# Both halves of the gated one-hot matrix on VectorE, in the gate stage of an S5 + mLSTM + PEER block

## The reference, cut to what matters

```
def peer(h, w_query, key1, key2, expert_u, expert_v):
    ...
    top_s, pos = lax.top_k(cand, PEER_TOPK)
    experts = jnp.take_along_axis(cand_idx, pos, axis=-1)
    gates = jax.nn.softmax(top_s, axis=-1).astype(h.dtype)
    def block(args):
        tb, eb, gb = args
        u = jnp.take(expert_u, eb, axis=0)
        act = jax.nn.gelu(jnp.einsum('ted,td->te', u, tb)) * gb
        vv = jnp.take(expert_v, eb, axis=0)
        return jnp.einsum('te,ted->td', act, vv)
```

## Time and profile before

| | us |
|---|---|
| median of 3 runs | 4708.28 |
| lowest and highest | 4703.58, 4708.52 |
| span of the profiled execution | 4703.4 |
| TensorE matmul busy | 4432.6 (94%) |
| VectorE busy | 2598.8 (55%) |
| ScalarE busy | 1247.2 (27%) |
| GpSimd busy | 1132.2 (24%) |

### The profile page before, as it was taken

The page is one execution under the profiler, slowest core; times in us unless marked ns, Lnnn a source line. Parts: engine busy times, 40 slices in busy tenths (PEclk is TensorE's granted clock), DMA queues, the critical chain, the costliest instruction groups (busy, mean ns, idle before and its releaser), DMA issues.

```text
span 4703.4 us, 56133 instructions
## 1 busy us (share of the span) xinstructions
PE 4432.6 (94%) x19304; PEld 3596.4 (76%) x19304; DVE 2598.8 (55%) x3702; ACT 1247.2 (27%) x1346; POOL 1132.2 (24%) x680
## 2 busy tenths in 40 slices
PE   7999999967898999999888899999999999999997
PEld 4886666755786788887777788888888888888886
DVE  5228888476533445449999555555533433333334
ACT  3232222343222222223333222222222222222222
POOL 1003444432112444547676200000000000000001
PEclk9999999978999999999999999999999999999999
DMA  2332222421433232233444544444333332333322
GB/s 113 128 114 101 91 92 102 169 75 42 169 139 138 83 114 107 103 118 139 154 143 149 216 146 149 141 149 143 133 116 107 111 109 101 116 107 107 115 91 89
DMA packets 101020, 567.75 MB, mean 121 GB/s; under 512 B 12056, under 2 KB 12072, under 8 KB 48864
## 3 DMA queue, kind: packets, MB, share of 16 engines
q1 hardware_dynamic: 55872, 406.87, 24.4%
q0 software_dynamic: 24352, 93.07, 6.4%
q10 hardware_dynamic: 20736, 67.12, 3.7%
HBM read 487.30 MB, written 79.72 MB: 121 GB/s over the span
## 4 chain that ended last, share of the span: by engine, by line
PE 64%; DVE 14%; PEld 10%; issue 8%; ACT 1%; POOL 1%; DMA 1%; DVEq 1%; PEldq 0%; ACTq 0%; POOLq 0%; SPq 0%
PE mm L1615 10%; PE mm L1616 10%; PE mm L1617 10%; PE pv L1615 5%; PE pv L1616 5%; PE pv L1617 5%; PE sc L1615 5%; PE sc L1616 5%; PE sc L1617 5%; PEld mm L1615 2%; PEld mm L1617 2%; PEld mm L1616 2%; DVE hot_j L1520 2%; DVE hot_jg L1525 2%; DVE gst L1535 1%
## 5 line engine op out<-in xcount | busy, mean ns | idle before, releaser
L618 ACT ACTIVATE whi<-raw 128x2048 fp32r<-128x2048 f32 x380 | 726.9, 1913 | 948.4 <-PE sc L1617 800.0
L990 DVE TENSOR_TENSOR wlo<-raw,whi 128x2048 fp32r<-128x2048 f32 x293 | 672.1, 2294 | 534.0 <-ACT whi L618 532.7
L1615 PE MATMUL mm<-t_hi,whi 128*128 128x512 f32 x2048 | 809.5, 395 | 63.8 <-POOL wlo L513 59.1
L1616 PE MATMUL mm<-t_lo,whi 128*128 128x512 f32 x2048 | 805.2, 393 | 0.0
L1617 PE MATMUL mm<-t_hi,wlo 128*128 128x512 f32 x2048 | 803.9, 393 | 0.0
L1615 PEld LDWEIGHTS mm<-t_hi,whi 128*128 128x128 f32 x2048 | 389.2, 190 | 149.7 <-issue 43.5
L513 POOL TENSOR_TENSOR wlo<-raw,whi 128x2048 fp32r<-128x2048 f32 x84 | 417.4, 4969 | 300.4 <-ACT whi L618 300.4
L1617 PEld LDWEIGHTS mm<-t_hi,wlo 128*128 128x128 f32 x2048 | 389.3, 190 | 82.5
L1616 PEld LDWEIGHTS mm<-t_lo,whi 128*128 128x128 f32 x2048 | 389.3, 190 | 79.0
L1615 PE MATMUL mm<-hn_hi,whi 128*128 128x512 f32 x960 | 380.3, 396 | 34.1 <-DVE hn_lo L1026 19.3
L1615 PE MATMUL pv<-act_hi,whi 128*128 (+1 forms) x1024 | 398.5, 389 | 2.6 <-DVE wlo L990 2.6
(11 more groups left out here) (347 smaller groups left out, 6853.9 us busy)
## 6 DMA issues: line engine op xcount, KB each, us to landing
raw<-stream SPq DMA_DIRECT2D x380, 1024.0 KB, 4.8
g_d<-gst ACTq DMA_DIRECT2D x16, 2048.0 KB, 7.2
gg<-g_d POOLq DMA_DIRECT2D x32, 1024.0 KB, 7.4
up_d<-sgl ACTq DMA_DIRECT2D x72, 256.0 KB, 2.0
gl<-up_d POOLq DMA_DIRECT2D x72, 256.0 KB, 2.9
spill<-stage ACTq DMA_DIRECT2D x56, 256.0 KB, 2.0
x<-xT SPq DMA_DIRECT2D x4, 1024.0 KB, 9.5
sa<-spill POOLq DMA_DIRECT2D x16, 256.0 KB, 3.1
```

Of the source, the lines that this page charges most:

```text
L618: act.activation(whi[:, k, :], raw[:, k, :], ACT.Copy).then_inc(hi_done, 1)
L990: dve.tensor_tensor(wlo[:, k, :], raw[:, k, :], whi[:, k, :].bitcast(F32), ALU.subtract)\
L1615: pe.matmul(out, lh, rh, start=start, stop=False)
L1616: pe.matmul(out, lh, rl, start=False, stop=False)
```

## The change: what it does, and the diff

GpSimd's `hot_low` goes. VectorE's `hot_rows` makes the low half of `hot_jg` itself, behind the high half, with the same operands and the same output. The two semaphores that told TensorE of the halves become one, raised behind the second. GpSimd's loop of the stage keeps only `next_lo`.

```diff
@@ gpsimd
-            pool.wait_ge(glo_done, 1)
-            lo_cols = gate_lo[:].rearrange("p (n w) -> p n w", w=8)
-
-            def hot_low(n, b):
-                pool.wait_ge(hotj_done, n + 1)
-                pool.tensor_tensor(hot_jg[:, b, :, 1, :], hot_j[:, b, :, :],
-                                   lo_cols[:, n, :].unsqueeze(2).to_broadcast([P, 8, P]), ALU.mult)\
-                    .then_inc(hotl_done, 1)
-
             with pool.Fori(0, 16) as r:
                 for s in range(2):
-                    for q in range(2):
-                        hot_low(4 * r + 2 * s + q, q)
                     next_lo(U_GATE // 2 + r, s)
@@ vector
+            lo_cols = gate_lo[:].rearrange("p (n w) -> p n w", w=8)
             dve.wait_ge(h2_out, 16)
+            dve.wait_ge(glo_done, 1)
...
                 dve.wait_ge(hotj_done, n8 + 1)
                 dve.tensor_tensor(hot_jg[:, b, :, 0, :], hot_j[:, b, :, :],
-                                  g_cols[:, n8, :].unsqueeze(2).to_broadcast([P, 8, P]), ALU.mult)\
-                    .then_inc(hoth_done, 1)
+                                  g_cols[:, n8, :].unsqueeze(2).to_broadcast([P, 8, P]), ALU.mult)
+                dve.tensor_tensor(hot_jg[:, b, :, 1, :], hot_j[:, b, :, :],
+                                  lo_cols[:, n8, :].unsqueeze(2).to_broadcast([P, 8, P]), ALU.mult)\
+                    .then_inc(hot_done, 1)
@@ tensor
-                        pe.wait_ge(hoth_done, 2 * n + q + 1)
-                        pe.wait_ge(hotl_done, 2 * n + q + 1)
+                        pe.wait_ge(hot_done, 2 * n + q + 1)
```

More of the change, by code:

```diff
@@ L254, in build @@
         tr_done, trc_done = sem("tr_done"), sem("trc_done")
-        glo_done, hotj_done, hoth_done, hotl_done = sem("glo_done"), sem("hotj_done"), sem("hoth_done"), sem("hotl_done")
+        glo_done, hotj_done, hot_done = sem("glo_done"), sem("hotj_done"), sem("hot_done")
         hot_used, gcopy_done, gps_free = sem("hot_used"), sem("gcopy_done"), sem("gps_free")
```

## The result

| | median us | runs | ratio to before, 95% interval |
|---|---|---|---|
| before | 4707.07 | 16 | |
| both halves on VectorE | 4716.29 | 16 | 1.002 [1.0012, 1.0027] |

The change makes the kernel 9.2 us slower, 0.20%. That is little, but the interval lies wholly on the slower side of 1, so it is a loss and not nothing. The forecast was 4710 in a range of 4695 to 4724.

A forecast was written before the change was run, and what follows sets the result against it. The prediction took VectorE as the gate stage's bound, part of its time stalled by GpSimd; +8 us in the stage and -6 behind it made +2, put on a 4708.28 us median as 4710, range 4695 to 4724.

The forecast's parts named there:

- signs of being right: Gate stage: hot_jg 1.2 us, wlo 4.5 to 5.6, turn 63.4, TensorE idle about 80 before L1855, no gap before L2.
- VectorE is the bound, and its stalls are the port: Gate stage: VectorE bounds; its two-SBUF-input instructions and GpSimd's TENSOR_TENSOR shut each other out, while gathers pass; turn 62.46 us.
- The removed stalls, -13.6 us a turn, and the added products, +9.1: Gate stage: 8 stalls behind hot_low go, -13.6 us a turn; 8 more VectorE instructions at 1.135 add +9.1.
- rival 3: Gate stage: hot_jg is slow by itself because it writes every second 128 columns; about 4890 us, chance 0.03.
- The new stalls behind wlo, 16.3 us a turn: Gate stage: first, second and fourth units stall 4.4 us each, third 3.07 under a gather; +5.8 a turn over before.
- rival 1: Gate stage: shorter stalls, wlo behaving like hot_low (-13) or first unit's wlo getting its gather (up to -10); about 4698, chance 0.17.
- it gets in at its end, ahead of the next one: Gate stage: GpSimd asking in mid VectorE two-SBUF-input instruction gets in when that ends, before VectorE's next; no size given.
- At the turn TensorE is no longer late, -0.3 us: Turn of the gate stage's loop: TensorE reaches hot 7 before rows 7 are done, giving back 0.3 us a turn.
- rival 2: Gate stage: TensorE's clock slows after waits before hot 0 and the fourth gather is lost; 4715 to 4727 us, chance 0.21.
- The stage +8: Gate stage: products, removed stalls, new stalls and the turn sum to +1.0 us a turn, +8 us over eight turns.
- Behind the stage, -6: After the gate stage: L2's load comes early, act_hi starts 7.4 us sooner, gl's reload loses 1.2; -6 us.
- Rival 4: Gate stage: wlo stops VectorE little, so 47 us a turn lies under TensorE's 52.3; -80 us, 4630, chance 0.03.

The follow-up runs named there:

- e1: The changed kernel with wlo of the gate stage made by VectorE behind each even group's gather, nothing of the stage on GpSimd: 4652.48 us.
- e2: The kernel before with wlo of the gate stage moved to VectorE and the low half of hot_jg still on GpSimd: 4686.82 us.
- e3: The changed kernel with one wait added, so GpSimd starts wlo when the rows of the unit's second group are done, under the gathers: 4680.39 us.
- e5: The changed kernel with VectorE's loop cut one group later, so the gathers of groups 6 and 7 no longer come together: 4699.49 us.
- e7: The changed kernel with the second gate load behind the gate stage issued after the two reloads of gl instead of before them: 4712.06 us.
- e4: The changed kernel with a wait added, so GpSimd starts wlo when the next group's first rows (hot_j) are done, beside rows without a gather: 4775.74 us.

## Why the prediction was right, point by point

The bound and the mechanism were right. The time came out near the top of the range: +9.2 us where the sum had +2, with both of its terms short, the stage by 5 us and the part behind it by 1.5. That the time lies in the range is the width of the range as well as the mechanism, and one of the stated signs of being wrong is there: a turn over 64.5 us (64.7 in the later turns, 64.3 in the mean of seven). Of the signs of being right three came only in part. TensorE idles 52.5 us before L1855 and 9.5 before a unit's first matmul, for 80 and none. VectorE's instruction of some 5.5 us is there in two units of four, for three. And `wlo` lasts up to 6.3 us, for 5.6.

- *VectorE is the bound, and its stalls are the port.* Held. The sum by instructions, gathers, stalls and waits gave the turn of e1 and e2 to 0.1 us before they ran (with no waits in either), and e3 gained 36 us from a wait that only shifts GpSimd.
- *The removed stalls, -13.6 us a turn, and the added products, +9.1.* Held: the high half takes 1.21 us where GpSimd is idle, and rival 3 (`hot_jg` slow by itself) fell with it.
- *The new stalls behind wlo, 16.3 us a turn.* Measured 15.3. The total came close, but none of the four came out as it was placed, and that the errors nearly cancelled is luck. In the order of the rows above:
  - The fourth unit's, at the turn (asked at 2314.33): I had the low product of the first rows stalled. It went ahead of `wlo`, and the next `hot_j` was stalled, 4.42 us for my 4.4.
  - The first unit's (2330.60): with that stall behind rows 0 and not in front of them, VectorE reached the end of gather 1 4.3 us later than in my placing and `wlo` came only 3.3 later, so that it found 1 us of the gather: 3.44 for my 4.4. This is the second half of rival 1.
  - The second unit's (2349.58, asked 0.49 us into the high product): the low product went ahead again, so that the stall had a gather over it, 3.09 for my 4.4.
  - The third unit's (2358.50): it was asked in the high product and not in the low one, and got in at its end, so that no gather lay over it, 4.36 for my 3.07.

  The step that failed is "it gets in at its end, ahead of the next one": in two of the four, VectorE's next product went first.
- *At the turn TensorE is no longer late, -0.3 us.* This is the term that was wrong, 2.4 us of waits in place of about 0.2. The stalled low product (2359.18) holds back gather 5, TensorE pauses in front of hot 6, and the clock falls. TensorE's hot weight loads of groups 6 and 7, and the stretches between:

```profile
2365.14 0.83 PEld L1855 LDWEIGHTS pv<-hot_jg,hot_i 128*128 128x128 f32 x4 [3.80 <-DVE gst L1528]
2373.02 0.65 PEld L1855 LDWEIGHTS pv<-hot_jg,hot_i 128*128 128x128 f32 x4
```
```profile
2362.00:2364.00 2.00, 0.00 (x0) 0.00 (x0) 2.00 (x1) 0.00 (x0) 1.67 (x1) 1.00 0.00 0
2364.00:2366.00 2.00, 0.86 (x4) 0.86 (x5) 2.00 (x6) 0.20 (x1) 0.00 (x0) 0.84 0.58 106
2366.00:2368.00 2.00, 2.00 (x9) 1.81 (x8) 2.00 (x3) 1.41 (x4) 0.00 (x0) 0.50 0.99 418
```

  From hot 6 to hot 7 TensorE takes 7.9 us instead of about 6.5, and it reaches hot 7 2.4 us after its rows are ready. With two gathers together at the turn nothing hides that. It is the mechanism of rival 2, at a place where I had not put it. Of the 2.4 us some 1.4 are the slower way from hot 6 to hot 7, an estimate from the two distances; the rest is that hot 6 itself came late, behind gather 5. In e5 the waits in the turn are gone.
- *The stage +8.* Its last hot matmul starts at 2633.3, before at 2619.9: +13. Eight turns of 2.2 us would be 17; the seven turns listed above differ by 3.4, 1.9, -1.3, 0.8, 3.6, 2.3 and 2.4 us. The third has no wait at its turn.
- *Behind the stage, -6.* From the last hot matmul to the first down matmul it was 55.3 us and is 50.8: -4.5. L2 no longer waits for its load, as forecast, and `act_hi` starts within 1.5 us of where it was placed. Under-sized was the reload of `gl` beside the second gate load: 7.06 us for 2.80, +4.3 where the bound was 2.4. e7 shows that this load is the cause.
- *The wlo that behaves like hot_low (rival 1).* Fell; of its two halves only the gather of the first unit came true, 1 us a turn. Where `wlo` gets in, it holds VectorE its full 4.4 us. For the length of the hold the trace agrees with the exclusive lock of the Trainium skill's page "SBUF — State Buffer", section "SBUF: two separate sides".
- *The price of rival 3,* 4890, was added up wrongly. The second product at 2.84 us and the stalls that would then not go are twice 13.6 us a turn, not 9.5 and 13.6, which gives some 4930. Nothing hangs on it, since `hot_jg` takes 1.21 us.
- *Rival 4, the stage becomes TensorE's,* did not come with the change. e1 is nearest to it: 55.7 us a turn, against 52.3 that TensorE needs.

## What to carry to other kernels

In all these runs a GpSimd TENSOR_TENSOR with inputs in SBUF was not beside VectorE's two-input work but in it. Price it as its length minus the VectorE instructions that pass, here those with an input in PSUM. Here 4.4 us of port on GpSimd stood for 2.2 us of work on VectorE, and taking the low halves off GpSimd lost 9 us while `wlo` stayed and started as soon as it could, and gained 34 once `wlo` had gone. Where an instruction must stay there, the moment at which it starts is worth as much as its length (4680 us in e3, 4776 in e4, which differ in where one wait stands): start it where passing work lies, and not so late that its reader waits.

## What the runs showed of the hardware that I had not expected

- Who gets the port next is not settled by who asked first. `hot_low`, asked 0.25 us into `hot_i`, got in at its end in all 64 cases (they last 2.71 to 2.73 us, all alike). In the changed kernel `wlo` asked 0.49 us into a 1.21 us product and let the next one pass (2349.58), and asked 0.46 us into one and got in (2358.50). In e4, with the ask always 0.25 us into `hot_i`, it got in at once (5.39 us) or behind three instructions (7.61 us), in the same place of the loop each turn. What decides it stays open.
- A load of 256 KB took 7.06 us beside one of 1 MB and 2.79 without it (e7), both loads from GpSimd's queue.
- After a pause of TensorE of 3.38 us, in front of the hot matmuls of group 6, the granted clock was at the lower of its two levels (1.2 GHz, 0.50 in 2366 to 2368). The length of the pause alone does not tell: in the kernel before, the clock stayed at 1.00 behind one of 2.65 us (2589.86) and was at 0.56 behind one of 2.67 (2605.78).
